# The last output tile's second product in two of 256 columns, a bank of its own for the last, and its closing scale-and-add shared by VectorE and GpSimd

## The chip, the cores and the metric

The kernel runs on the eight cores of one Trainium2 chip. Each core owns 2,048 of the 16,384 token positions and runs the same program; the cores exchange nothing. The metric is the device time of the slowest core in microseconds (us): 961.11 us is the median of three runs of the kernel before (960.91 to 961.43). The trace is one execution taken on the slowest core, which took 961.42 us in all, with a span of 959.5 us from its first to its last instruction.

## The reference

One decoder layer: a gated mixing sub-layer, then a SwiGLU feed-forward layer. The change is in the very last piece, the feed-forward layer's down projection with its normalisation and residual:

```python
def rms_norm(x, g):
    xf = x.astype(jnp.float32)
    y = xf * lax.rsqrt(jnp.mean(xf * xf, axis=-1, keepdims=True) + EPS) * g
    return y

h2 = rms_norm(x, g_pre_ffn[l])
gu = h2 @ w_gate_up[l]                       # 1024 -> 2 * 2816
a, b = gu[..., :FFN_HIDDEN], gu[..., FFN_HIDDEN:]
x = x + rms_norm((jax.nn.silu(a) * b) @ w_down[l], g_post_ffn[l])   # 2816 -> 1024
```

## The kernel before

A program written in Python lists the operations of each engine; a list scheduler with estimated costs then fixes their order and puts the waits between engines (`Prog`, its `schedule` and `emit`). Every instruction is issued from one of two lines of a helper, 521 and 523, so the rows of the trace are told apart by the names of their tiles.

The core's 2,048 positions are 16 tiles of 128. The last phase runs twice, for 8 tiles at a time: `gate_up` makes the hidden activations `ffT` (22 blocks of 128 features), then `down` makes one output tile at a time. A tile of `down` is 128 positions by 1,024 columns, made as two products of 512 columns, each a sum of 22 matmuls (`mm8` with `nk=NJ`; 16 of them take their columns from `wdna`, 6 from `wdnb`), in two neighbouring banks of PSUM, a pair from the ring `any2`. There are four such pairs.

For every tile but the last, ScalarE squares the 1,024 columns and sums them (`junkd<-ps`, then a read of the accumulator), takes a square root (`st<-st`), and VectorE multiplies the product by the gain (`x1b<-ps,gfin`), takes the reciprocal of the root and ends with one instruction that scales and adds the residual (`x1b<-x1b,st,xin`). SyncE (SP) then issues the store of 128 x 1,024 float32 values (512 KB).

For the last tile (lines 1394 to 1413) this is done in halves of 512 columns. ScalarE squares a half as soon as its product is there, VectorE multiplies it by the gain; after the second half come the square root, with the first half's sum as its bias, the reciprocal, and two scale-and-add instructions of 512 columns, columns 512 to 1,023 first. Each is followed by a store of 256 KB from SP. Nothing follows these stores: SP waits for all of the open ones and the program ends.

GpSimd (POOL) has nothing to do in the last eight tiles: its last instruction is an issue of a load of weights for `gate_up`. The scheduler's own costs hold an account of a port that VectorE and GpSimd use in turn (`n.port` in `call`, `earliest`), which sets the order only.

Of the kernel before, what the change touches and what calls it, by code (L numbers as in the profile page):

```python
# [8 lines left out]
AF = mybir.ActivationFunctionType  # L9
ALU = mybir.AluOpType  # L10
# [3 lines left out]
D = 1024  # L14
T = S // NCORES
NT = T // 128
FF = 2816
NJ = FF // 128
EPS = 1e-6
KB = 1024  # L20

MERGE_AT = 1
STATS_TO = 8
POOL_ALL = 16
FLIGHT = 5
# [547 lines left out]
def build_program():  # L573
# [26 lines left out]
    out_d = nc.dram_tensor("out", [T, D], F32, kind="ExternalOutput").ap()  # L600
# [3 lines left out]
    pe, act, dve, pool, sp = P.pe, P.act, P.dve, P.pool, P.sp  # L604
# [4 lines left out]
    def singles(ids):  # L609
        return Ring(P, [ps[:, b, :] for b in ids], [(bank[b],) for b in ids], False)  # L610

    def pairs(ids, fifo=False):
        return Ring(P, [ps[:, b:b + 2, :] for b in ids], [(bank[b], bank[b + 1]) for b in ids], fifo)

    any1, any2 = singles(range(8)), pairs([0, 2, 4, 6])
# [5 lines left out]
    def take(nbytes):  # L621
        nonlocal o
        r = o
        o += (nbytes + 31) // 32 * 32
        return r
# [15 lines left out]
    st = P.ring("st", [128, 2], F32, [take(8) for _ in range(16)], False)  # L641
# [61 lines left out]
    dsem = P.new_proc  # L703
# [64 lines left out]
    for what in LOADS:  # L768
# [17 lines left out]
        else:  # L786
            g = int(what[1])
# [25 lines left out]
    def rstd(src, junk_ring, after, by_dve=False, by_pool=False, by_act=False):  # L813

        s_, j = st.new(), junk_ring.new()
        if by_dve:
            sq = dve.scalar_tensor_tensor(out=j[:, :], in0=src, scalar=1.0, in1=src, op0=ALU.mult, op1=ALU.mult, accum_out=s_[:, 0:1], after=after)
        else:
            sq = act.activation(out=j[:, :], in_=src, func=AF.Square, accum_out=s_[:, 0:1], after=after)
        j.free(sq)  # L820
        if by_pool:
            e = pool.tensor_scalar(out=s_[:, 0:1], in0=s_[:, 0:1], scalar1=D * EPS, scalar2=None, op0=ALU.add, after=[sq])
            s_.tok = pool.tensor_tensor(out=s_[:, 1:2], in0=s_[:, 0:1], in1=nhalf[:, :], op=ALU.pow, after=[e, m_half])
        elif by_act:
            e = act.activation(out=s_[:, 0:1], in_=s_[:, 0:1], func=AF.Ln, scale=1.0, bias=D * EPS, after=[sq])
            s_.tok = act.activation(out=s_[:, 1:2], in_=s_[:, 0:1], func=AF.Exp, scale=-0.5, after=[e])
        else:
            e = act.activation(out=s_[:, 0:1], in_=s_[:, 0:1], func=AF.Sqrt, scale=1.0, bias=D * EPS, after=[sq])
            s_.tok = dve.reciprocal(out=s_[:, 1:2], in_=s_[:, 0:1], after=[e])
        return s_, sq  # L830
# [18 lines left out]
    def mm8(out, lhs, rhs, nk=8, after=(), claim=()):  # L849
        with pe.group(after) as n:  # L850
            for t in claim:
                n.tiles.append(t)
                n.after.update(t.ring.follow)
            for k in range(nk):
                pe.matmul(out, lhs(k), rhs(k), start=(k == 0), stop=(k == nk - 1))
        return n
# [117 lines left out]
    def norm_tile(i):  # L974
        halo = i >= NT
        P.bias = PART["norm_h" if halo else "norm"]
        if i % 2 == 0:
            pair[:] = [xt.pop(0), xt.pop(0)]
            sums, sqs = st4.new(), []
            for e, u in enumerate(pair):  # L980
                if e == 1 and i < STATS_TO:

# [50 lines left out]
    for g in range(4):  # L1033
        c, hf = g // 2, g % 2
# [16 lines left out]
    for c in range(2):  # L1051
        b = any1.new()
# [229 lines left out]
    for s in range(4):  # L1282
# [6 lines left out]
        pooled(s, fill1)  # L1289
        if s == MERGE_AT:  # L1290
            P.bias = PART["m01"]
# [10 lines left out]
    gfin = P.sb("gfin", [128, D], F32, R4 + 20 * KB)  # L1302
# [3 lines left out]
    junkd = P.ring("junkd", [128, D], BF16, [R3 + 32 * KB + i * 2 * KB for i in range(2)], False, follow=att_all)  # L1306
    wgu = P.ring("wgu", [128, 2, 8, 128], BF16, [R5 + i * 4 * KB for i in range(3)], follow=w01_pool)
    ffT = P.sb("ffT", [128, NJ, 1024], BF16, R2)
    wdn_a = P.sb("wdna", [128, 16, D], BF16, R1)
    wdn_b = P.sb("wdnb", [128, 6, D], BF16, R4)  # L1310
# [6 lines left out]
    v_gfin = dve.tensor_scalar(out=gfin[:, :], in0=gfin[:, :], scalar1=32.0, scalar2=None, op0=ALU.mult, after=[d_gfin])  # L1317
# [27 lines left out]
    ff_w = {0: [], 1: []}  # L1345
# [22 lines left out]
    out_evs = []  # L1368

    def down(i):  # L1370
        il = i % 8
        r = slice(i * 128, (i + 1) * 128)
        xi = xin.new()
        xi.tok = sp.dma(xi[:, :], x1s_d[r, :], after=[x1_ev[i]])
        b = any2.new()
        ms = []
        for h2 in range(2):
            ms.append(mm8(b[:, h2, :], lambda j: ffT[:, j, il * 128:(il + 1) * 128],
                          lambda j: wdn_a[:, j, h2 * 512:(h2 + 1) * 512] if j < 16 else wdn_b[:, j - 16, h2 * 512:(h2 + 1) * 512], nk=NJ, after=ff_w[i // 8] + d_wdn))
        dn_mm[i // 8].extend(ms)  # L1380
        x1 = x1b.new()
        if i < NT - 1:
            y = b.ap.rearrange("p a b -> p (a b)")
            rs, sq = rstd(y, junkd, ms, by_pool=i < NT // 2)
            g = dve.tensor_tensor(out=x1[:, :], in0=y, in1=gfin[:, :], op=ALU.mult, after=[sq, v_gfin])
            b.free(sq, g)
            w = dve.scalar_tensor_tensor(out=x1[:, :], in0=x1[:, :], scalar=rs[:, 1:2], in1=xi[:, :], op0=ALU.mult, op1=ALU.add, after=[rs.tok, g, xi.tok])
            out_evs.append(sp.dma(out_d[r, :], x1[:, :], after=[w]))
            rs.free(w)
            xi.free(w)  # L1390
            x1.free(out_evs[-1])
            return

        j, s_ = junkd.new(), [st.new(), st.new()]
        sq, g, w = [], [], []
        for h2 in range(2):
            c = slice(h2 * 512, (h2 + 1) * 512)
            sq.append(act.activation(out=j[:, c], in_=b[:, h2, :], func=AF.Square, accum_out=s_[h2][:, 0:1], after=[ms[h2]]))
            g.append(dve.tensor_tensor(out=x1[:, c], in0=b[:, h2, :], in1=gfin[:, c], op=ALU.mult, after=[sq[h2], v_gfin]))
            if h2 == 0:  # L1400
                e = dve.tensor_scalar(out=s_[0][:, 1:2], in0=s_[0][:, 0:1], scalar1=D * EPS, scalar2=None, op0=ALU.add, after=[sq[0]])
        b.free(*sq, *g)
        j.free(*sq)
        q = act.activation(out=s_[1][:, 0:1], in_=s_[1][:, 0:1], func=AF.Sqrt, scale=1.0, bias=s_[0][:, 1:2], after=[sq[1], e])
        p = dve.reciprocal(out=s_[1][:, 1:2], in_=s_[1][:, 0:1], after=[q])
        s_[0].free(q)
        for h2 in (1, 0):
            c = slice(h2 * 512, (h2 + 1) * 512)
            w.append(dve.scalar_tensor_tensor(out=x1[:, c], in0=x1[:, c], scalar=s_[1][:, 1:2], in1=xi[:, c], op0=ALU.mult, op1=ALU.add, after=[p, g[h2], xi.tok]))
            out_evs.append(sp.dma(out_d[r, c], x1[:, c], dsem("d_out%d" % h2), after=[w[-1]]))  # L1410
        s_[1].free(*w)
        xi.free(*w)
        x1.free(*out_evs[-2:])

    for i in range(NT):
        out_proj(i)
# [1 line left out]
    d_wdn = []  # L1418
    for i in range(11):
        j = 2 * i  # L1420
        dst = wdn_a[:, j:j + 2, :] if j < 16 else wdn_b[:, j - 16:j - 14, :]
        d_wdn.append(pool.dma(dst, wdn_d[:, j:j + 2, :], dsem("d_wd%d" % i), after=[wgu_n[2 * i]] + (out_mm[i // 2] if j < 16 else sum(out_mm.values(), []))))
    for i in range(8):
        down(i)
    gate_up(1)
    for i in range(8, 16):
        down(i)
# [117 lines left out]
```

How the kernel before makes its waits and increments, by code:

```python
    def emit(self):  # L480
# [19 lines left out]
                if e.seen.get(proc, 0) >= val:  # L500
                    continue
                e.seen[proc] = val
                snap = self.procs[proc].snaps.get(val)
                if snap:
                    for k, v in snap.items():
                        if e.seen.get(k, 0) < v:
                            e.seen[k] = v
                s = self.procs[proc].sem
                e.meta.append(("wait", proc, val))
                e.ops.append(lambda q, s=s, val=val: q.wait_ge(s, val))
            sem, step = (sem, 16) if n.dma else (e.proc, 1)
            sem.count += step
            n.tick = (sem.idx, sem.count)
# [2 lines left out]
            res = lambda a: a.resolve() if isinstance(a, View) else a  # L516
            for j, (method, args, kw) in enumerate(n.items):
                a = [res(x) for x in args]
                k = {q: res(x) for q, x in kw.items()}
                if j == len(n.items) - 1:
                    e.ops.append(lambda q, m=method, a=a, k=k, s=sem.sem, v=step: getattr(q, m)(*a, **k).then_inc(s, v))
                else:
                    e.ops.append(lambda q, m=method, a=a, k=k: getattr(q, m)(*a, **k))
# [1 line left out]
    def finish(self, last):  # L525
        e, need = self.sp, {}
        for n in last:
            need[n.tick[0]] = max(need.get(n.tick[0], 0), n.tick[1])
        for p, v in need.items():
            if e.seen.get(p, 0) < v:
                e.meta.append(("wait", p, v))
                e.ops.append(lambda q, s=self.procs[p].sem, v=v: q.wait_ge(s, v))
```

## Time and profile before

| | |
|---|---|
| median of three runs | 961.11 us (960.91 to 961.43) |
| the profiled execution | 961.42 us, span 959.5 us, so 1.9 us lie outside the span |
| spans of the eight cores | 955.7 to 959.5 us, mean granted clock 0.994 to 0.998 |
| busy share of the span | PE 98%, VectorE 42%, GpSimd 36%, ScalarE 34% |
| chain that ended last | PE 85%, transfers 4%, the rest 3% or less each |
| last matmul starts / last scale-and-add ends / span ends | 953.49 / 957.10 / 959.5 us |

Shares of busy time tell little here, since the change touches the last ten microseconds. What matters is the sequence of single instructions in the timeline from 948 us on: which instruction starts when, and how long after the one that it waits for.

### The profile page before, as it was taken

The numbers are of one execution on the slowest core, as the hardware profiler recorded it, in microseconds if no ns is written. First come the engines' busy times: TensorE is split into PE (matmuls) and PEld (weight loads), VectorE is DVE, ScalarE is ACT, GpSimd is POOL, SyncE is SP. The second block draws the span as 40 slices with busy tenths as digits, with TensorE's granted clock in tenths as the row PEclk, the third lists the DMA queues.
The fourth block names the chain that finished last, engine by engine and source line by source line (L and its number), as shares of the span: only waits on it lengthen the run. The fifth ranks groups of instructions, "written<-read, shape, count | busy, mean of one in ns | idle before, by whom it ended". The sixth has DMA issues, their size and how long they took to land.

```text
span 959.5 us, 15261 instructions; the slowest of 8 cores (955.7 to 959.5 us)
## 1 busy us (share of the span) xinstructions
PE 936.4 (98%) x5629; PEld 478.1 (50%) x5629; DVE 400.7 (42%) x529; ACT 321.5 (34%) x537; POOL 349.4 (36%) x358
## 2 busy tenths in 40 slices
PE   8899999999999999999999999999999999999997
PEld 4466877655554543444444444444444444444443
DVE  4578846768834653334563112221222222211323
ACT  3257524463425653234772111111011111111211
POOL 2679964467764437436891110100000000000000
PEclk9989999999999999999999999999999999999999
DMA  8996521321043228734877656652325354440221
GB/s 191 183 257 190 190 68 45 56 57 24 2 66 67 45 34 135 196 75 113 282 252 161 110 102 125 119 101 66 117 102 132 66 87 67 84 71 1 90 108 66
DMA packets 30761, 103.21 MB, mean 108 GB/s; under 512 B 4064, under 2 KB 4064, under 8 KB 30688
## 3 DMA queue, kind: packets, MB, share of 16 engines
q0 software_dynamic: 14432, 45.65, 28.9%
q1 hardware_dynamic: 15856, 56.50, 17.6%
q8 instruction: 46, 0.75, 0.3%
q14 instruction: 27, 0.22, 0.1%
q10 hardware_dynamic: 400, 0.08, 0.1%
HBM read 131.09 MB, written 16.78 MB: 154 GB/s over the span
## 4 chain that ended last, share of the span: by engine, by line
PE 85%; DMA 4%; issue 3%; ACT 3%; DVE 3%; POOL 2%; DVEq 0%; POOLq 0%; ACTq 0%; SPq 0%
PE ps L523 75%; PE ps L521 10%; DMA wgs<-wg 1%; DMA wq<-wq 1%; DMA wk<-wk 1%; DMA terms<-terms 1%; POOL x1b L521 1%; ACT PT L521 1%; DVE PT L521 1%; POOL st L521 1%; ACT L521 1%; ACT junkd L521 0%; ACT tg L521 0%; DVE x1b L521 0%; ACT den L521 0%
## 5 line engine op out<-in xcount | busy, mean ns | idle before, releaser
L523 PE MATMUL ps<-hT,wgu 128*128 128x512 bf16 x1232 | 294.6, 379 | 0.0
L523 PEld LDWEIGHTS ps<-hT,wgu 128*128 128x128 bf16 x1232 | 120.4, 98 | 144.4
L521 DVE TENSOR_TENSOR ffT<-ps,sa 128x512 bf16<-128x512 f32 x88 | 60.8, 691 | 228.9 <-PE ps L521 226.6
L521 ACT ACTIVATE sa<-ps 128x512 f32<-128x512 f32 x88 | 52.5, 596 | 238.7 <-PE ps L521 238.7
L523 PE MATMUL ps<-wdna,ffT 128*128 128x512 bf16 x512 | 115.7, 379 | 1.0 <-issue 0.6
L521 POOL DMA_DIRECT2D wgu<-wgu x44 | 23.6, 537 | 243.4 <-PE ps L521 243.4
L523 PE MATMUL ps<-hT,wgs 128*128 128x512 bf16 x448 | 108.1, 382 | 3.7 <-ACT tg L521 1.4
L521 DVE TENSOR_TENSOR rt<-ps,tab 128x512 f32<-128x512 f32 (+1 forms) x120 | 75.4, 669 | 33.7 <-PE ps L521 17.2
L523 PEld LDWEIGHTS ps<-wdna,ffT 128*128 128x128 bf16 x512 | 50.0, 98 | 61.9 <-issue 2.0
L521 ACT ACTIVATE junkd<-ps 128x1024 bf16<-128x1024 f32 (+1 forms) x33 | 32.7, 991 | 142.8 <-PE ps L521 142.7
L521 DVE SCALAR_TENSOR_TENSOR tg<-tg,ps 128x512 f32<-128x512 f32 x64 | 43.7, 686 | 75.8 <-ACT tg L521 67.5
L523 PEld LDWEIGHTS ps<-hT,wgs 128*128 128x128 bf16 x448 | 43.1, 98 | 57.0 <-issue 7.3
L521 POOL TENSOR_TENSOR k<-rt 128x512 bf16<-128x512 f32 (+1 forms) x36 | 64.9, 1817 | 17.4 <-DVE rt L521 17.0
L521 DVE TENSOR_TENSOR x1b<-ps,gfin 128x1024 f32<-128x1024 f32 (+1 forms) x17 | 19.7, 1162 | 116.9 <-ACT junkd L521 116.9
L521 PE MATMUL ps<-hT,wgu 128*128 128x512 bf16 x176 | 66.7, 379 | 0.0
L521 ACT ACTIVATE tg<-ps 128x512 f32<-128x512 f32 x64 | 38.1, 597 | 79.1 <-PE ps L521 79.0
L521 POOL TENSOR_TENSOR mT<-tg 128x512 bf16<-128x512 f32 x32 | 41.6, 1301 | 49.7 <-DVE tg L521 49.5
L521 POOL TENSOR_TENSOR q<-rt 128x512 bf16<-128x512 f32 x24 | 47.7, 2002 | 30.5 <-DVE rt L521 30.5
L521 ACT ACTIVATE PT<-ps 128x1024 bf16<-128x1024 f32 x48 | 48.8, 1022 | 28.5 <-PE ps L521 28.2
L521 DVE TENSOR_TENSOR PT<-PT,masks 128x1024 bf16<-128x1024 bf16 x48 | 46.7, 984 | 23.5 <-ACT PT L521 23.3
L523 PE MATMUL ps<-wout,mT 128*128 128x512 bf16 x224 | 53.6, 379 | 0.4 <-DVE x1b L521 0.4
L521 ACT ACTIVATE v<-ps 128x256 bf16<-128x256 f32 x69 | 26.3, 383 | 76.2 <-PE ps L521 75.8
(143 smaller groups left out, 1261.0 us busy)
## 6 DMA issues: line engine op xcount, KB each, us to landing
wgu<-wgu POOLq DMA_DIRECT2D x44, 512.0 KB, 5.2
xst<-xo SPq DMA_DIRECT2D x16, 512.0 KB, 8.5
xsth<-xh SPq DMA_DIRECT2D x16, 512.0 KB, 5.2
wgs<-wg POOLq DMA_DIRECT2D x16, 512.0 KB, 5.6
xin<-xo SPq DMA_DIRECT2D x16, 512.0 KB, 5.8
x1s<-x1b SPq DMA_DIRECT2D x16, 512.0 KB, 4.0
xin<-x1s SPq DMA_DIRECT2D x16, 512.0 KB, 4.1
out<-x1b SPq DMA_DIRECT2D x15, 512.0 KB, 2.9
```

Source lines behind the costliest of these rows:

```text
L521: e.ops.append(lambda q, m=method, a=a, k=k, s=sem.sem, v=step: getattr(q, m)(*a, **k).then_inc(s, v))
L523: e.ops.append(lambda q, m=method, a=a, k=k: getattr(q, m)(*a, **k))
```

## The change

The last tile is cut into 512, 256 and 256 columns. The products of the first two lie in the tile's pair of banks, the third in a single bank from the ring `any1`. ScalarE squares each cut apart and VectorE multiplies each by the gain; the three partial sums are added by two one-column operations and by the bias of the square root. After the reciprocal, GpSimd scales columns 0 to 191 (a `tensor_scalar`) and adds the residual (a `tensor_tensor`); VectorE does columns 608 to 1,023 and then 192 to 607 by the scale-and-add instruction, 416 columns each. There are three stores: 208 KB, 208 KB and 96 KB, issued in this order, the one of GpSimd's columns last.

```diff
+LAST_POOL = 192
...
-        for h2 in range(2):
-            ms.append(mm8(b[:, h2, :], lambda j: ffT[:, j, il * 128:(il + 1) * 128],
-                          lambda j: wdn_a[:, j, h2 * 512:(h2 + 1) * 512] if j < 16 else wdn_b[:, j - 16, h2 * 512:(h2 + 1) * 512], nk=NJ, after=ff_w[i // 8] + d_wdn))
+        cuts = [(0, 512), (512, 1024)] if i < NT - 1 else [(0, 512), (512, 768), (768, 1024)]
+        y = b.ap.rearrange("p a b -> p (a b)")
+        b2 = any1.new() if i == NT - 1 else None
+        at = [y[:, c0:c1] if c0 < 768 else b2[:, 0:256] for c0, c1 in cuts]
+        for o_, (c0, c1) in zip(at, cuts):
+            ms.append(mm8(o_, lambda j: ffT[:, j, il * 128:(il + 1) * 128],
+                          lambda j: wdn_a[:, j, c0:c1] if j < 16 else wdn_b[:, j - 16, c0:c1], nk=NJ, after=ff_w[i // 8] + d_wdn))
...
-        for h2 in range(2):
-            c = slice(h2 * 512, (h2 + 1) * 512)
-            sq.append(act.activation(out=j[:, c], in_=b[:, h2, :], func=AF.Square, accum_out=s_[h2][:, 0:1], after=[ms[h2]]))
-            g.append(dve.tensor_tensor(out=x1[:, c], in0=b[:, h2, :], in1=gfin[:, c], op=ALU.mult, after=[sq[h2], v_gfin]))
-            if h2 == 0:
+        for n, (c0, c1) in enumerate(cuts):
+            c = slice(c0, c1)
+            sq.append(act.activation(out=j[:, c], in_=at[n], func=AF.Square, accum_out=s_[n][:, 0:1], after=[ms[n]]))
+            g.append(dve.tensor_tensor(out=x1[:, c], in0=at[n], in1=gfin[:, c], op=ALU.mult, after=[sq[n], v_gfin]))
+            if n == 0:
                 e = dve.tensor_scalar(out=s_[0][:, 1:2], in0=s_[0][:, 0:1], scalar1=D * EPS, scalar2=None, op0=ALU.add, after=[sq[0]])
+            if n == 1:
+                e = dve.tensor_tensor(out=s_[1][:, 1:2], in0=s_[1][:, 0:1], in1=s_[0][:, 1:2], op=ALU.add, after=[sq[1], e])
...
-        q = act.activation(out=s_[1][:, 0:1], in_=s_[1][:, 0:1], func=AF.Sqrt, scale=1.0, bias=s_[0][:, 1:2], after=[sq[1], e])
-        p = dve.reciprocal(out=s_[1][:, 1:2], in_=s_[1][:, 0:1], after=[q])
-        for h2 in (1, 0):
-            c = slice(h2 * 512, (h2 + 1) * 512)
-            w.append(dve.scalar_tensor_tensor(out=x1[:, c], in0=x1[:, c], scalar=s_[1][:, 1:2], in1=xi[:, c], op0=ALU.mult, op1=ALU.add, after=[p, g[h2], xi.tok]))
-            out_evs.append(sp.dma(out_d[r, c], x1[:, c], dsem("d_out%d" % h2), after=[w[-1]]))
+        q = act.activation(out=s_[2][:, 0:1], in_=s_[2][:, 0:1], func=AF.Sqrt, scale=1.0, bias=s_[1][:, 1:2], after=[sq[2], e])
+        p = dve.reciprocal(out=s_[2][:, 1:2], in_=s_[2][:, 0:1], after=[q])
+        c = slice(0, LAST_POOL)
+        pa = pool.tensor_scalar(out=x1[:, c], in0=x1[:, c], scalar1=s_[2][:, 1:2], scalar2=1.0, op0=ALU.mult, op1=ALU.mult, after=[p, g[0]])
+        w.append(pool.tensor_tensor(out=x1[:, c], in0=x1[:, c], in1=xi[:, c], op=ALU.add, after=[pa, xi.tok]))
+        mid = (1024 + LAST_POOL) // 2
+        for c0, c1 in ((mid, 1024), (LAST_POOL, mid)):
+            c = slice(c0, c1)
+            w.append(dve.scalar_tensor_tensor(out=x1[:, c], in0=x1[:, c], scalar=s_[2][:, 1:2], in1=xi[:, c], op0=ALU.mult, op1=ALU.add, after=[p] + g + [xi.tok]))
+        for n, (c0, c1) in ((1, (mid, 1024)), (2, (LAST_POOL, mid)), (0, (0, LAST_POOL))):
+            out_evs.append(sp.dma(out_d[r, c0:c1], x1[:, c0:c1], dsem("d_out%d" % n), after=[w[n]]))
```

The order of all engines is the same in both kernels up to the last tile. VectorE's last rows stand so before (`x1b` is the output tile, `st` the sums, `xin` the residual, `p_scalar`, `p_vector` and `p_gpsimd` the counters of ScalarE, VectorE and GpSimd):

```order
L521 TENSOR_TENSOR x1b_113_155<-ps,gfin_147 128x512 [waits p_scalar,r84]
L521 TENSOR_SCALAR st_25_67<-st_25_67 128x1
L521 TENSOR_TENSOR x1b_113_155<-ps,gfin_147 128x512 [waits p_scalar]
L521 RECIPROCAL st_12_54<-st_12_54 128x1 [waits p_scalar]
L521 SCALAR_TENSOR_TENSOR x1b_113_155<-x1b_113_155,st_12_54,xin_109_151 128x512 [waits p_vector,r80]
L521 SCALAR_TENSOR_TENSOR x1b_113_155<-x1b_113_155,st_12_54,xin_109_151 128x512
```

And so after the change:

```order
L522 TENSOR_TENSOR x1b_113_155<-ps,gfin_147 128x512 [waits p_scalar,r85]
L522 TENSOR_SCALAR st_25_67<-st_25_67 128x1
L522 TENSOR_TENSOR x1b_113_155<-ps,gfin_147 128x256 [waits p_scalar]
L522 TENSOR_TENSOR st_12_54<-st_12_54,st_25_67 128x1 [waits p_vector]
L522 TENSOR_TENSOR x1b_113_155<-ps,gfin_147 128x256 [waits p_scalar]
L522 RECIPROCAL st_11_53<-st_11_53 128x1 [waits p_scalar]
L522 SCALAR_TENSOR_TENSOR x1b_113_155<-x1b_113_155,st_11_53,xin_109_151 128x416 [waits p_vector,r81]
L522 SCALAR_TENSOR_TENSOR x1b_113_155<-x1b_113_155,st_11_53,xin_109_151 128x416
```

The second gain product is in two pieces with a one-column add between them, and the two closing instructions have 416 columns in place of 512. On GpSimd two instructions of 192 columns follow its last load; the first waits for VectorE's counter, the second for GpSimd's own.

SP's last rows before, with its closing wait at the branch (`d_out0` and `d_out1` are the counters of the last tile's stores, `r81` to `r83` those of earlier tiles):

```order
L521 DMA out<-x1b_110_152 128x1024 [waits p_vector]
L521 DMA out<-x1b_111_153 128x1024 [waits p_vector]
L521 DMA out<-x1b_112_154 128x1024 [waits p_vector]
L521 DMA out<-x1b_113_155 128x512 [waits p_vector] x2
L563 UNCONDITIONAL_BRANCH [waits r81,r82,r83,d_out1,d_out0]
```

And after the change:

```order
L522 DMA out<-x1b_110_152 128x1024 [waits p_vector]
L522 DMA out<-x1b_111_153 128x1024 [waits p_vector]
L522 DMA out<-x1b_112_154 128x1024 [waits p_vector]
L522 DMA out<-x1b_113_155 128x416 [waits p_vector] x2
L522 DMA out<-x1b_113_155 128x192 [waits p_gpsimd]
L564 UNCONDITIONAL_BRANCH [waits r82,r83,r84,d_out1,d_out2,d_out0]
```

The third store stands behind the two of VectorE's columns in SP's queue, whichever engine is done first.

## Rows read from the trace of the kernel before

**Rows 1.** Timeline, 948 to 960 us: start, us, engine, line, operation [idle before].

```profile
948.95 3.62 PE L523 MATMUL ps<-wdna,ffT 128*128 128x512 bf16 x16
...
953.49 0.38 PE L521 MATMUL ps<-wdnb,ffT 128*128 128x512 bf16 x1
953.96 0.60 ACT L521 ACTIVATE junkd<-ps 128x512 bf16<-128x512 f32 x1 [4.06 <-PE ps L521]
954.46 0.19 ACT L521 ACTIVATION_READ_ACCUMULATOR junkd<-ps 128x1 f32 x1
954.74 0.29 ACT L521 ACTIVATE st<-st,st 128x1 f32<-128x1 f32 x1
954.75 0.69 DVE L521 TENSOR_TENSOR x1b<-ps,gfin 128x512 f32<-128x512 f32 x1 [3.93 <-ACT junkd L521]
955.36 0.15 DVE L521 RECIPROCAL st<-st 128x1 f32<-128x1 f32 x1
955.69 1.41 DVE L521 SCALAR_TENSOR_TENSOR x1b<-x1b,st,xin 128x512 f32<-128x512 f32 x2 [0.17 <-DVE st L521]
956.52 0.99 SPq L521 DMA_DIRECT2D out<-x1b  x2
```

**Rows 2.** Timeline of PE, 117 to 122 us: products of 256 columns, 8 matmuls each.

```profile
117.29 0.93 PE L523 MATMUL ps<-wv,hTh 128*128 128x256 bf16 x7
...
120.79 0.93 PE L523 MATMUL ps<-wv,hTh 128*128 128x256 bf16 x7
```

**Rows 3.** Stretches: busy of PE, PEld, DVE, ACT, POOL, then granted clock, DMA.

```profile
55.60:59.90 4.30, 4.30 (x36) 3.72 (x35) 1.29 (x2) 2.47 (x6) 4.30 (x3) 0.81 0.91 256
950.00:955.00 5.00, 3.87 (x18) 1.57 (x16) 1.00 (x3) 0.94 (x3) 0.00 (x0) 1.00 0.14 56
```

**Rows 4.** Groups by shape, whole span: busy us, mean ns | idle before.

```profile
L521 ACT ACTIVATE v<-ps 128x256 bf16<-128x256 f32 x69 | 26.3, 383 | 76.2 <-PE ps L521 75.8 <-issue 0.2
L521 DVE SCALAR_TENSOR_TENSOR x1b<-x1b,st,xin 128x1024 f32<-128x1024 f32 x15 | 19.3, 1284 | 3.1 <-DVE x1b L521 1.9 <-DVE st L521 1.2
L521 DVE SCALAR_TENSOR_TENSOR x1b<-x1b,st,xin 128x512 f32<-128x512 f32 x2 | 1.4, 747 | 0.2 <-DVE st L521 0.2
L521 POOL TENSOR_SCALAR xsb<-xsth,st 128x1024 bf16<-128x1024 f32 x16 | 17.7, 1120 | 1.2 <-ACT st L521 1.0
L521 POOL TENSOR_TENSOR x1b<-x1b,xin 128x1024 f32<-128x1024 f32 x16 | 37.4, 2351 | 4.0 <-DVE x1b L521 4.0
L521 POOL TENSOR_TENSOR k<-rt 128x128 bf16<-128x128 f32 x2 | 0.9, 450 | 1.9 <-DVE rt L521 1.9
```

**Rows 5.** Timeline of VectorE and GpSimd, 198 to 226 us.

```profile
198.29 0.17 DVE L521 TENSOR_TENSOR uZ<-uZ,small 64x16 f32<-64x16 f32 x1
...
208.30 1.06 POOL L521 TENSOR_TENSOR uY<-uX 128x527 f32<-128x527 f32 x1 [1.26 <-DVE zT L521]
209.04 0.35 DVE L521 TENSOR_TENSOR uZ<-uZ,small 64x16 f32<-64x16 f32 x1
...
221.21 2.26 POOL L521 TENSOR_TENSOR q<-rt 128x512 bf16<-128x512 f32 x1
221.60 2.42 DVE L521 TENSOR_TENSOR PT<-PT,masks 128x1024 bf16<-128x1024 bf16 x1
```

**Rows 6.** Timeline, 276 to 278 and 661 to 663 us: when GpSimd starts.

```profile
276.62 0.69 DVE L521 SCALAR_TENSOR_TENSOR tg<-tg,ps 128x512 f32<-128x512 f32 x1 [0.20 <-ACT tg L521]
277.46 1.26 POOL L521 TENSOR_TENSOR mT<-tg 128x512 bf16<-128x512 f32 x1 [1.00 <-DVE tg L521]
...
661.33 0.22 POOL L521 TENSOR_SCALAR st<-st 128x1 f32<-128x1 f32 x1 [12.30 <-ACT junkd L521]
...
661.70 0.57 POOL L521 TENSOR_TENSOR st<-st,nhalf 128x1 f32<-128x1 f32 x1
```

**Rows 7.** DMA issues: count, KB each, median us from issue to landing.

```profile
out<-x1b SPq DMA_DIRECT2D x15, 512.0 KB, 2.9
out<-x1b SPq DMA_DIRECT2D x2, 256.0 KB, 2.1
```

More of the change, by code:

```diff
@@ L1382, in down @@
         if i < NT - 1:
-            y = b.ap.rearrange("p a b -> p (a b)")
             rs, sq = rstd(y, junkd, ms, by_pool=i < NT // 2)
@@ L1392, in down @@
             return
-        j, s_ = junkd.new(), [st.new(), st.new()]
+        j, s_ = junkd.new(), [st.new(), st.new(), st.new()]
         sq, g, w = [], [], []
-        for h2 in range(2):
-            c = slice(h2 * 512, (h2 + 1) * 512)
-            sq.append(act.activation(out=j[:, c], in_=b[:, h2, :], func=AF.Square, accum_out=s_[h2][:, 0:1], after=[ms[h2]]))
-            g.append(dve.tensor_tensor(out=x1[:, c], in0=b[:, h2, :], in1=gfin[:, c], op=ALU.mult, after=[sq[h2], v_gfin]))
-            if h2 == 0:
+        for n, (c0, c1) in enumerate(cuts):
[3 more added lines that the diff above has]
+            if n == 0:
@@ L1401, in down @@
                 e = dve.tensor_scalar(out=s_[0][:, 1:2], in0=s_[0][:, 0:1], scalar1=D * EPS, scalar2=None, op0=ALU.add, after=[sq[0]])
-        b.free(*sq, *g)
+            if n == 1:
+                e = dve.tensor_tensor(out=s_[1][:, 1:2], in0=s_[1][:, 0:1], in1=s_[0][:, 1:2], op=ALU.add, after=[sq[1], e])
+        b.free(*sq[:2], *g[:2])
+        b2.free(sq[2], g[2])
         j.free(*sq)
-        q = act.activation(out=s_[1][:, 0:1], in_=s_[1][:, 0:1], func=AF.Sqrt, scale=1.0, bias=s_[0][:, 1:2], after=[sq[1], e])
@@ L1405, in down @@
-        p = dve.reciprocal(out=s_[1][:, 1:2], in_=s_[1][:, 0:1], after=[q])
-        s_[0].free(q)
-        for h2 in (1, 0):
-            c = slice(h2 * 512, (h2 + 1) * 512)
-            w.append(dve.scalar_tensor_tensor(out=x1[:, c], in0=x1[:, c], scalar=s_[1][:, 1:2], in1=xi[:, c], op0=ALU.mult, op1=ALU.add, after=[p, g[h2], xi.tok]))
-            out_evs.append(sp.dma(out_d[r, c], x1[:, c], dsem("d_out%d" % h2), after=[w[-1]]))
-        s_[1].free(*w)
+        q = act.activation(out=s_[2][:, 0:1], in_=s_[2][:, 0:1], func=AF.Sqrt, scale=1.0, bias=s_[1][:, 1:2], after=[sq[2], e])
@@ new lines, in down @@
+        p = dve.reciprocal(out=s_[2][:, 1:2], in_=s_[2][:, 0:1], after=[q])
+        s_[0].free(e)
+        s_[1].free(q)
+        c = slice(0, LAST_POOL)
[5 more added lines that the diff above has]
+            w.append(dve.scalar_tensor_tensor(out=x1[:, c], in0=x1[:, c], scalar=s_[2][:, 1:2], in1=xi[:, c], op0=ALU.mult, op1=ALU.add, after=[p] + g + [xi.tok]))
@@ L1412, in down @@
+        for n, (c0, c1) in ((1, (mid, 1024)), (2, (LAST_POOL, mid)), (0, (0, LAST_POOL))):
+            out_evs.append(sp.dma(out_d[r, c0:c1], x1[:, c0:c1], dsem("d_out%d" % n), after=[w[n]]))
+        s_[2].free(*w)
         xi.free(*w)
-        x1.free(*out_evs[-2:])
+        x1.free(*out_evs[-3:])
     for i in range(NT):
```

## The prediction

> **What bounds the kernel now.** I read the stretches first: from 950 to 955 us PE is busy to the last matmul, at a granted clock of 1.00, the level of 2.4 GHz [rows 3]. So the last tile starts when PE comes to it, and nothing that is changed lies ahead of that. Then I read the timeline of the end, where every step is a wait for the step before [rows 1]. The second product's 22 matmuls start at 948.95 and the last of them at 953.49, 4.54 / 21 = 0.216 us apart; it takes 0.38 us, and ScalarE starts its square at 953.96, 0.09 us after that end. The accumulator is read 0.50 us after the start of the square. From this read the square root starts 0.28 us later and VectorE's gain product 0.29 us later, side by side. The reciprocal starts at 955.36, 0.08 us before the gain product's end at 955.44 and long after the root's end at 955.03, so VectorE's own queue sets it. It ends at 955.51, and 0.18 us later the two scale-and-add instructions start; they end at 957.10. SP issues the first store at 956.52, which is 0.08 us after the first of them (0.747 us, [rows 4]) has ended at 956.44, and the second one the same 0.08 us after 957.10, at 957.18. SP is done at 957.51, so an issue takes 0.33 us. A store of 256 KB lands 2.1 us after its issue [rows 7], at 959.28. From the last matmul to that landing there are 5.4 us of bare waiting, and these are what the change works on. I set its sum against 959.28 in this execution of 961.42 us, which is 0.31 us above the median of 961.11.
>
> **The change part by part.**
>
> *The product in two.* 22 matmuls of 512 columns become 44 of 256. Five products of 256 columns with 8 matmuls each ran back to back early in the kernel: the first began at 117.29, the fifth at 120.79, so 32 matmuls took 3.50 us, 0.1094 us each [rows 2]. Half of 0.216 is 0.108, so the weight load before each matmul stays hidden and little is lost. The last of the 44 starts 43 x 0.1094 = 4.70 us after 948.95, at 953.65. A matmul of 512 columns takes 0.38 us from its start, of 256 columns about 0.11 less, 0.27, so the sum is there at 953.92 in place of 953.87: 0.05 us lost. The middle product's square, gain product and one-column add have the 2.4 us of the third product to run in; the matching work on the first half takes from 953.96 to 955.44 when nothing hides it [rows 1], so they cost nothing. Without that cover they would cost their 1.5 us. The third product's bank was used by one of the tiles before, whose reads end microseconds earlier.
>
> *The last square and gain product.* With 256 columns ScalarE takes 0.383 us [rows 4] against 0.60: 0.22 less. Square from 954.01, accumulator read at 954.01 + 0.50 - 0.22 = 954.29, gain product at 954.58, root from 954.57 to 954.86. VectorE's price per column is (1284 - 747) / 512 = 1.05 ns [rows 4], so its product takes 0.69 - 0.27 = 0.42 us and ends at 955.00. The reciprocal could start at 954.92 by VectorE's queue, but the root's end at 954.86 plus the 0.10 us that VectorE takes to hear ScalarE (954.65 to 954.75, [rows 1]) makes it 954.96. It ends at 955.11, 0.40 us earlier than before. From here on I count from 955.11.
>
> *The shared end.* VectorE's instruction of 416 columns takes 0.747 - 0.10 = 0.65 us, two in a row 0.56 + 0.65. GpSimd's two are shown at no width of 192. The scale lies between 0.21 us (192/1024 of 1.120) and 0.39 (0.22 for one column plus 191 x 0.88 ns) [rows 4, 6]; I take 0.39, since a fixed part is plain in the one-column row. The add lies between 0.44 us (192/1024 of 2.351) and 0.59 (0.45 for 128 columns plus 64 x 2.12 ns) [rows 4]; I take 0.59, since 128 is the nearest width. GpSimd starts 0.15 us after an instruction of VectorE that it waits for (277.31 to 277.46), and 0.15 us after one of its own (661.55 to 661.70) [rows 6]. The scale could thus start at 955.26 and VectorE's first instruction at 955.11 + 0.18 = 955.29.
>
> They can't run together. At 209.04 VectorE starts an instruction with two inputs in SBUF while GpSimd works: it takes 0.35 us where the same takes 0.17, and ends 0.03 us after GpSimd's 209.36. At 221.60 another takes 2.42 us and ends 0.55 us after the GpSimd instruction that was running, at 223.47 [rows 5]. Such an instruction waits for the whole GpSimd instruction, apart from some 0.13 us of its beginning. And at 221.21 GpSimd, waiting for a VectorE instruction, went ahead of the next one of VectorE's queue, which was started at 221.60 [rows 5]. So whoever has waited goes next. The scale-and-add reads `x1b` and `xin`, both in SBUF, so it is such an instruction, and the two engines take turns.
>
> The Trainium skill, GPSIMD Engine Reference, section Key points, says that GpSimd shares its SBUF interfaces with VectorE and contends with VectorE instructions that have two SBUF inputs; these rows agree. By that rule alone the end is the one with turns below, without it the one without turns.
>
> With GpSimd first: scale 955.26 to 955.65; VectorE's first ends 0.52 later at 956.17; GpSimd's add, ready at 955.80, ends 0.59 - 0.14 = 0.45 later, at 956.62; VectorE's second ends at 957.14. SP issues the second store at 957.22 and the third, which stands behind it, 0.33 later at 957.55. With VectorE first: 955.94, scale 956.20, second 956.72, add 957.17; second store at 956.80, third at 957.25. The starts are 0.03 us apart, which decides nothing, so I take both orders as one case.
>
> *The stores.* The third has 96 KB. By the step from 512 to 256 KB (0.8 us less, [rows 7]) it would land in 2.1 - 0.5 = 1.6 us; it can hardly take more than the 2.1 of 256 KB. I take 1.8. It lands at 957.55 + 1.8 = 959.35 or at 959.05, against 959.28: +0.07 or -0.23, and with the bounds of the landing -0.43 to +0.37. The second store, with 208 KB, would land by the same step at 957.22 + 1.95 = 959.17, before the third.
>
> *Sum:* +0.05 for the product, -0.45 for square, gain product and the earlier reciprocal, and then a shorter VectorE end that is given back by the turns and by a third issue on SP. The middle of the two orders is -0.08 us: 961.34 against 961.42, and 961.0 against the median. The forecast is no change that can be measured; 0.2%, 1.9 us here, is about what a measurement of this kernel can tell from no change.
>
> **The rivals.**
>
> *No turns.* If instructions of this kind don't exclude each other, VectorE ends at 955.29 + 0.56 + 0.65 = 956.50 and GpSimd at 955.26 + 0.39 + 0.15 + 0.59 = 956.39. The second store goes at 956.58, the third at 956.91, and lands at 958.71: 0.57 us faster, 960.5. For it: none of my rows has a float32 scale-and-add of this form beside GpSimd. Against it: the 0.35 us row is float32 with two inputs in SBUF, and the rule is plain in it.
>
> *The product slows down.* The matmuls of 256 columns could fall to a lower granted clock in the last tile. Its place is 951 to 954 us. Where products of 256 columns ran at a granted 0.81 [rows 3], the price per matmul is 0.1094 / 0.81 = 0.135 us, 0.026 more, and 44 of them add 1.1 us: 962.1, slower than before. At the level of 1.2 GHz it would be 4.8 us: 965.8, a slowdown that is measurable. It decides as soon as the granted clock between 949 and 954 us is under about 0.98, where 44 x 0.002 us takes up the gain of 0.08. For it: it did happen at 55.6. Against it: there it was in the first tenth of the run, and here the clock is 1.00 up to the end.
>
> *The change doesn't do what it says.* The order shows the 44 matmuls, the two GpSimd instructions and the three stores, in their places. I give this nothing.
>
> **How the numbers follow.** Turns on the port 0.78 (961.0, and 960.7 to 961.5 by its own bounds), no turns 0.14 (960.5), a slower product 0.08, of which 0.03 at the level of 1.2 GHz. Runs of the kernel before differ by 0.5 us among themselves, so I add 0.3 us on either side of the cases that I take in: 960.3 to 961.8. Faster by over 0.2% needs a gain of 1.9 us, and no case has it: 0.01. Slower by over 0.2%: 0.03. The rest, 0.96, is within.
>
> **What would show it.** In the timeline after: 44 matmuls 0.109 us apart; the last square some 0.38 us long; the reciprocal about 0.4 us closer to the start of the second product; then one scale-and-add, or GpSimd's scale, longer than its 0.65 or 0.39 us by the other's time, and a third store issued 3.6 to 3.9 us after the last matmul's start (here 953.65). It is wrong if both engines' closing instructions keep their plain durations side by side, if the matmuls stand 0.13 us apart, or if the third store's landing takes more than 2.1 us.

## The result and the profile after

The changed kernel takes 967.47 us (median of four runs, 967.15 to 968.95) against 961.01 us before: a ratio of 1.0067, 95% interval 1.0056 to 1.0079. It is slower by 6.5 us, where no measurable change (961.0, range 960.3 to 961.8) was forecast. Medians of one kernel move by about a microsecond from one measuring session to the next, so every comparison below goes by the ratio to the kernel before in the same session, or by one core's trace. The ratios leave out executions in which the cores of a die showed a lower granted clock and the time was longer.

The timeline of the changed kernel's end, on its slowest core (start us, us, engine, line, operation; all line numbers are one higher than before):

```profile
948.55 1.91 PE L524 MATMUL ps<-wdna,ffT 128*128 128x256 bf16 x16
...
953.25 0.27 PE L522 MATMUL ps<-wdnb,ffT 128*128 128x256 bf16 x1
953.62 0.38 ACT L522 ACTIVATE junkd<-ps 128x256 bf16<-128x256 f32 x1 [1.93 <-PE ps L522]
953.90 0.20 ACT L522 ACTIVATION_READ_ACCUMULATOR junkd<-ps 128x1 f32 x1
954.19 0.29 ACT L522 ACTIVATE st<-st,st 128x1 f32<-128x1 f32 x1
954.20 0.42 DVE L522 TENSOR_TENSOR x1b<-ps,gfin 128x256 f32<-128x256 f32 x1 [1.91 <-ACT junkd L522]
954.58 0.16 DVE L522 RECIPROCAL st<-st 128x1 f32<-128x1 f32 x1
954.92 1.30 DVE L522 SCALAR_TENSOR_TENSOR x1b<-x1b,st,xin 128x416 f32<-128x416 f32 x2 [0.17 <-DVE st L522]
954.93 0.86 POOL L522 TENSOR_SCALAR x1b<-x1b,st 128x192 f32<-128x192 f32 x1 [98.33 <-DVE st L522]
955.65 1.47 SPq L522 DMA_DIRECT2D out<-x1b  x3
955.99 0.67 POOL L522 TENSOR_TENSOR x1b<-x1b,xin 128x192 f32<-128x192 f32 x1 [0.21 <-POOL x1b L522]
```

These rows answer to [rows 1], and up to GpSimd's end they are close to what was forecast. The product of columns 512 to 1,023, now in two parts, starts at 948.55; the reciprocal comes 954.58 - 948.55 = 6.03 us after that, where it came 955.36 - 948.95 = 6.41 us after it: 0.38 us earlier, forecast 0.40. GpSimd ends at 956.66. The three stores land after these times (KB each, median us from issue to landing, to be read beside [rows 7]):

```profile
out<-x1b SPq DMA_DIRECT2D x2, 208.0 KB, 1.9
out<-x1b SPq DMA_DIRECT2D x1, 96.0 KB, 1.8
```

The last issue ends at 955.65 + 1.47 = 957.12 and so starts near 956.75; it lands 1.8 us later, at 958.5, which is 5.3 us after the last matmul's start. Before it was 5.8; yet the last matmul starts 4.70 us after the start of the product, where it was 4.54, so only 0.3 us of the 0.5 are gained. But the span ends at 965.3. The table of SP's waits (what was waited for: us in total, times, longest) shows that the time is lost after the stores:

```profile
SPq L564 <- PEq L564: 6.7, 1, 6.7
SPq L534 <- DMA out<-x1b: 1.1, 3, 0.6
```

SP waits 1.1 us for the stores and then 6.7 us at line 564, where the program's end is built. In the kernel before that wait was 0.2 us:

```profile
SPq L563 <- PEq L563: 0.2, 1, 0.2
```

The engine named there, PE, had long been done; which one it really was stands in the instructions of that line (operation: shortest/median/longest ns, first and last start us). After the change:

```profile
L564 POOLq EVENT_SEMAPHORE  x2: 17/17/17, 965.1 to 965.2; - x2
L564 PEldq DRAIN  x1: 2155/2155/2155, 951.4 to 951.4; - x1
L564 ACTq DRAIN  x1: 306/306/306, 954.2 to 954.2; - x1
L564 DVEq DRAIN  x1: 1282/1282/1282, 955.0 to 955.0; - x1
L564 POOLq DRAIN  x1: 9119/9119/9119, 956.0 to 956.0; - x1
L564 SPq DRAIN  x1: 7/7/7, 958.6 to 958.6; - x1
L564 SPq EVENT_SEMAPHORE  x1: 17/17/17, 965.3 to 965.3; - x1
```

And in the kernel before, at its line 563:

```profile
L563 POOLq EVENT_SEMAPHORE  x2: 17/17/17, 959.3 to 959.4; - x2
L563 POOLq DRAIN  x1: 9410/9410/9410, 856.5 to 856.5; - x1
L563 SPq DRAIN  x1: 7/7/7, 959.3 to 959.3; - x1
```

At the program's end a DRAIN instruction stands in the queue of every engine, and the engines meet when all of them are through (the EVENT_SEMAPHORE rows). In these traces GpSimd's closing drain starts together with its last instruction. Before, that was a load of weights, 103 us before the end, and the drain of 9.4 us lay beside PE's matmuls of `gate_up`. Now the last instruction is the add at 955.99; the drain takes 9.12 us from there, on this core as on all others within 2 ns, which is the add's own 0.67 us and 8.45 us more, and the engines of the core meet at 965.1. The drain didn't appear with the change: it was pulled to the end by it.

### The profile page after: what moved, and what is told of

The parts are those of the page before. It is cut to its first block, busy times and chain, and to the rows that moved or that the text cites. A ratio compares the mean times of both kernels' runs of the same rounds, so it can differ in the third digit from the quotient of the medians.

```text
span 965.3 us, 15227 instructions; the slowest of 8 cores (958.4 to 965.3 us)
## 1 busy us (share of the span) xinstructions
PE 927.6 (96%) x5557; PEld 478.5 (50%) x5651; DVE 402.8 (42%) x531; ACT 321.7 (33%) x539; POOL 351.4 (36%) x360
## 3 DMA queue, kind: packets, MB, share of 16 engines
q0 software_dynamic: 14432, 45.65, 28.9%
## 4 chain that ended last, share of the span: by engine, by line
PE 79%; DMA 6%; issue 5%; ACT 4%; POOL 3%; DVE 3%; POOLq 0%; ACTq 0%; DVEq 0%; SPq 0%
PE ps L524 69%; PE ps L522 10%; DMA wq<-wq 2%; DMA wv<-wv 1%; DMA wk<-wk 1%; DMA wgs<-wg 1%; POOL x1b L522 1%; ACT PT L522 1%; DVE PT L522 1%; POOL st L522 1%; DMA xst<-xo 1%; ACT L522 1%; POOL xsb L522 1%; ACT junk L522 0%; ACT junkd L522 0%
## 5 line engine op out<-in xcount | busy, mean ns | idle before, releaser
L524 PE MATMUL ps<-hT,wgu 128*128 128x512 bf16 x1203 | 290.8, 379 | 1.2
L524 PE MATMUL ps<-wdna,ffT 128*128 128x512 bf16 (+1 forms) x517 | 115.2, 372 | 1.5 <-issue 0.6
L522 ACT ACTIVATE junkd<-ps 128x1024 bf16<-128x1024 f32 (+2 forms) x34 | 32.9, 967 | 142.3 <-PE ps L522 142.3
L522 DVE TENSOR_TENSOR x1b<-ps,gfin 128x1024 f32<-128x1024 f32 (+2 forms) x18 | 19.9, 1106 | 116.1 <-ACT junkd L522 116.1
L522 PE MATMUL ps<-hT,wgu 128*128 128x512 bf16 x176 | 66.7, 379 | 0.3
```

The source lines that it names most:

```text
L522: e.ops.append(lambda q, m=method, a=a, k=k, s=sem.sem, v=step: getattr(q, m)(*a, **k).then_inc(s, v))
L524: e.ops.append(lambda q, m=method, a=a, k=k: getattr(q, m)(*a, **k))
```

## The experiments

The theory, **A**: the 6.5 us are GpSimd's drain, which follows its last instruction and can now hide behind nothing. The rivals: **B**, the products of 256 columns or the third bank cost it; **C**, the turns at the port and the third store do.

How long each kernel's slowest core takes from the start of its last matmul to the end of its span, beside the ratio to the kernel before:

| kernel | last matmul to end, us | ratio, 95% interval |
|---|---|---|
| before | 6.0 | |
| changed | 12.1 | 1.0067 (1.0056 to 1.0079) |
| without GpSimd's part | 5.5 | 0.9985 (0.9975 to 0.9996) |
| before, tiny instruction late | 10.2 | 1.0036 (1.0022 to 1.0049) |
| before, the same early | 6.1 | 0.9999 (0.9988 to 1.0009) |
| changed, end without the drain | 5.6 | 0.9989 (0.9978 to 1.0001) |
| before, end without the drain | 6.1 | 0.9998 (0.9983 to 1.0013) |
| without GpSimd's part and drain | 5.6 | 0.9988 (0.9974 to 1.0002) |
| changed, one more drain early | 5.7 | 0.9985 (0.9971 to 0.9999) |
| changed, one more drain halfway | 5.5 | one run of each: 959.35 beside 960.62 us |

Where the product is in two, the last matmul starts 0.16 us later after the product's start than before. So 0.16 us of what such a kernel has less than the 6.0 in the middle column is no gain.

**Without GpSimd's part.**

```diff
-        pa = pool.tensor_scalar(out=x1[:, c], ...)
-        w.append(pool.tensor_tensor(out=x1[:, c], ...))
...
-        for c0, c1 in ((mid, 1024), (LAST_POOL, mid)):
...
-            w.append(dve.scalar_tensor_tensor(out=x1[:, c], ...))
-        for n, (c0, c1) in ((1, (mid, 1024)), (2, (LAST_POOL, mid)), (0, (0, LAST_POOL))):
-            out_evs.append(sp.dma(out_d[r, c0:c1], ...))
+        for n, (c0, c1) in ((1, (512, 1024)), (0, (0, 512))):
+            w.append(dve.scalar_tensor_tensor(out=x1[:, c0:c1], ...))
+            out_evs.append(sp.dma(out_d[r, c0:c1], x1[:, c0:c1], dsem("d_out%d" % n), after=[w[-1]]))
...
```

> The products in 256 columns and the separate bank stay; GpSimd's two instructions go, VectorE does both closing halves of 512 columns, two stores of 256 KB. Theory A (the 6.5 us are GpSimd's drain at the end of the program, which now starts only after GpSimd's last instruction): GpSimd's drain lies around 856 us again and is over long before the end, and the time is 960.5 to 960.7 us, 0.3 to 0.5 us under the kernel before. Theory B (the shorter matmuls or the third bank cost the time): it stays near 967 us. Theory C (the exchange of the port between VectorE and GpSimd and the third store cost it): near 961 us, so this run alone does not tell A from C.

It is 0.15% faster than the kernel before (960.40 us beside 961.49), 1.4 us by the ratio with an interval of 0.4 to 2.4, where 0.3 to 0.5 was expected. Its end (instructions of line 564, then the last matmul in the timeline):

```profile
L564 POOLq DRAIN  x1: 9399/9399/9399, 857.5 to 857.5; - x1
L564 SPq DRAIN  x1: 7/7/7, 960.0 to 960.0; - x1
```

```profile
954.68 0.27 PE L522 MATMUL ps<-wdnb,ffT 128*128 128x256 bf16 x1
```

B falls: the 44 matmuls and the third bank are all in here. The drain is back at 857 us. SP is done 960.0 - 954.68 = 5.3 us after the last matmul's start. A and C are not told apart yet.

**A tiny GpSimd instruction, late and early.** The kernel before with one instruction of one column on GpSimd, which nobody reads or waits for:

```diff
         s_[0].free(q)
+        t_ = st.new()
+        t_.free(pool.tensor_scalar(out=t_[:, 0:1], in0=nhalf[:, :], scalar1=D * EPS, scalar2=None, op0=ALU.add, after=[sq[1], m_half]))
```

In the second kernel it is released by `sq[0]`, the square of the first half.

> The kernel before, with one GpSimd instruction of one column added, released by the last square; nothing reads its result, no engine waits for it, the stores are unchanged. Theory A: it runs about 1.0 us after the last matmul's start plus 0.2, so GpSimd's drain ends about 8.5 us later, some 4 us after the last store has landed: the time is 964.5 to 965.5 us. Theories B and C: no change, 961.0 us within 0.3.

> The same added instruction, but released by the square of the first half, 4.7 us earlier. Theory A: the drain ends 8.5 us after it, at or just before the landing of the last store, so the time is that of the kernel before, 961.0 to 961.3 us. If the mere presence of a late GpSimd instruction cost a fixed time wherever it stands, it would be as slow as the one released late.

Late, it costs 0.36% (964.96 us beside 961.49); early, nothing. In the kernel with the late one (timeline, then the instructions of its line 563):

```profile
956.50 0.38 PE L521 MATMUL ps<-wdnb,ffT 128*128 128x512 bf16 x1
957.83 0.22 POOL L521 TENSOR_SCALAR st<-nhalf 128x1 f32<-128x1 f32 x1 [97.81 <-ACT junkd L521]
```

```profile
L563 POOLq DRAIN  x1: 8681/8681/8681, 957.8 to 957.8; - x1
L563 SPq DRAIN  x1: 7/7/7, 962.3 to 962.3; - x1
```

SP is done with the stores at 962.3, and the drain ends at 957.83 + 8.68 = 966.5. With the early one:

```profile
949.91 0.22 POOL L521 TENSOR_SCALAR st<-nhalf 128x1 f32<-128x1 f32 x1 [93.06 <-ACT junkd L521]
```

```profile
L563 POOLq DRAIN  x1: 8681/8681/8681, 949.9 to 949.9; - x1
L563 SPq DRAIN  x1: 7/7/7, 959.1 to 959.1; - x1
```

The drain is as long, 8.46 us after the instruction's 0.22, but ends at 958.6, half a microsecond before SP is done. One instruction of 0.2 us that no one waits for costs 3.5 us (4.2 in the trace: 10.2 in place of 6.0) in one place and nothing 4.7 us earlier. This is A alone; there is no sharing, no third store and no shorter matmul in these kernels.

**The end without the drain.** Both kernels, with the engines meeting by semaphores and GpSimd not drained:

```diff
-        with nc.Block() as block:
+        with nc.Block(no_gpsimd_drain=True) as block:
```

> The changed kernel, every instruction kept, but the program's end is built without GpSimd's drain: the engines meet by semaphores alone. Theory A: the 6.5 us go, and what is left is the sum of the prediction's own parts: 960.3 to 960.8 us. Theories B and C: it stays at 967 us.

> The kernel before, with the program's end built without GpSimd's drain. Its drain of 9.4 us lies at 856 us and is over 93 us before the end, so Theory A says no change: 961.0 to 961.5 us, the same as the kernel before within 0.1%. If it were faster by a microsecond or more, the gain of the changed kernel without the drain would be the option's own and not the drain's.

The changed kernel falls from 1.0067 to 0.9989; the kernel before stays at 0.9998. So the option brings nothing of its own, and the whole loss of the change goes with the drain. At the end of the changed kernel without it (timeline, then its line 564):

```profile
954.89 0.27 PE L522 MATMUL ps<-wdnb,ffT 128*128 128x256 bf16 x1
```

```profile
L564 POOLq EVENT_SEMAPHORE  x2: 17/17/17, 960.3 to 960.4; - x2
L564 SPq DRAIN  x1: 7/7/7, 960.2 to 960.2; - x1
```

SP is done 5.3 us after the last matmul's start, as in the kernel without GpSimd's part. C falls, since the turns and the third store are all in here; but so does the use of sharing: it brings nothing over VectorE alone that these traces can show.

**Without GpSimd's part and without the drain.** This joins the edits of the first and of the last experiment.

> Products of 256 columns, no GpSimd work at the end, two stores, and the program's end without GpSimd's drain. Theory A: the same as with the drain, since that lies at 857 us: 960.4 to 960.8 us, 0.3 to 0.6 us under the kernel before. It shows what of the gain is left to the shared end: the changed kernel without the drain has its last landing 5.3 us after the last matmul's start, this one should have 5.5.

The ratio is 0.9988, with an interval that just holds 1. Its end (timeline, then its line 564):

```profile
954.33 0.27 PE L522 MATMUL ps<-wdnb,ffT 128*128 128x256 bf16 x1
```

```profile
L564 SPq DRAIN  x1: 7/7/7, 959.6 to 959.6; - x1
```

SP is done 5.3 us after the last matmul's start, where 5.5 was expected: with and without the sharing the stores are in at the same time. The kernel isn't told apart from the other three with the new products and no long drain left at the end (called repaired below), 0.9985 to 0.9989.

**One more drain, early and halfway.** What is the 8.4 us? The changed kernel with a drain of its own on GpSimd where it has nothing else to do:

```diff
     gate_up(1)
+    dr = pool.drain(after=[wgu_n[-1]])
```

(The scheduler's own cost for a drain, added in this kernel and the next one, is left out here.)

> The changed kernel with one more GpSimd drain in its program, behind the last load of weights that GpSimd issues, some 90 us before the end, where GpSimd has nothing else to do; the drain at the end stays. Theory A1 (the drain's 8.46 us wait for or clear what GpSimd's own transfers have left since the last drain): the second drain is a few tenths of a us long, like the 0.17 us of the one at the program's start, and the time is 960.5 to 961.0 us. Theory A2 (each drain of GpSimd costs 8.46 us once the program has issued transfers from it): no change against the changed kernel, 967 us.

The extra drain and the one at the end (instructions of lines 524 and 566 on the slowest core):

```profile
L524 POOLq DRAIN  x1: 8396/8396/8396, 864.5 to 864.5; - x1
...
L566 POOLq DRAIN  x1: 764/764/764, 959.2 to 959.2; - x1
```

The drain at the end is down to 0.764 us, 0.09 more than the add that it stands behind, and the kernel is at 0.9985. A1 holds, with a correction: the extra drain starts at 864.5, when the last load (issued at 859.3, 5.2 us to its landing) has landed, and still takes 8.4 us. So these 8.4 us are no wait for a landing. What the drain does in them no run shows. Whether they go with the number of transfers is asked by a kernel with the drain put before `gate_up(1)`:

```diff
+    dr = pool.drain(after=[wgu_n[21]] + d_wdn)
+    dr.prio = -1
     gate_up(1)
```

> The changed kernel with the extra drain of GpSimd put earlier, behind 81 of the 102 transfers that GpSimd issues, so that 21 are issued after it and have long landed at the end. If the drain's price goes with the number of transfers since the last drain (8.4 us for 102, 0.083 us each), the extra drain takes 6.7 us and the one at the end 1.7 us after the last add, which hides behind the last store: about 960.7 us. If it is one price however many there were, both take 8.4 us after what stands before them and the time is 967 us.

```profile
L524 POOLq DRAIN  x1: 7427/7427/7427, 634.4 to 634.4; - x1
...
L566 POOLq DRAIN  x1: 2497/2497/2497, 954.9 to 954.9; - x1
```

The drain at the end takes 2.497 - 0.67 = 1.83 us after the add, with 21 transfers since the last drain. With none it was 0.09, with all 102 it was 8.45: (1.83 - 0.09) / 21 = 0.083 us and (8.45 - 0.09) / 102 = 0.082 us for each. The price goes with the number of transfers, in one run of this kernel, whose eight cores agree within 1 ns on the 2.497 us. It doesn't go with their bytes. The page of this run has GpSimd's queue (packets, MB, share of the DMA engines' time):

```profile
q0 software_dynamic: 14432, 45.65, 28.6%
```

The 21 carry 512 KB each, 11.0 of these 45.65 MB, and by that share the drain would have taken 2.11 us after the add. Whether it is the transfers or the packets they are made of isn't told apart. The extra drain was to take 6.7 us and took 7.4, on other cores 7.2 to 8.8; it started when a load issued at 633.3 was still under way, and how much of it is waiting for that isn't separated.

## Why the prediction was wrong

The step that failed is the first one: "From the last matmul to that landing there are 5.4 us of bare waiting, and these are what the change works on. I set its sum against 959.28 ..." It took the landing of the last store for the end of the program. The sum thus has no term for what the program does between its last instructions and its end, and on GpSimd that is a drain of 8.4 us. The move of GpSimd's last instruction from 856 to 956 us was put at nothing, without a reason: it takes away the cover of everything that follows that instruction on its engine, and I named no such thing. What I wrote of the kernel before has the same gap: "Nothing follows these stores" and "Every instruction is issued from one of two lines of a helper" leave out the drains and semaphores of line 563. The evidence lay in the trace of before, in the instructions of that line; I read the end from the timeline, which shows no drains, and read GpSimd's queue only up to its last instruction. No rival held it: the slower one was a slower product, and the chance left for a measurable slowdown was 0.03. Of the three signs of being wrong that I named none came; none of them looked behind the stores.

The terms that were in the sum, counted from the last matmul's start:

- The product in two: the matmuls are (953.25 - 948.55) / 43 = 0.109 us apart, as worked out. Right. The granted clock was 1.00 in the stretches 940 to 950 and 950 to 955 us, the level of 2.4 GHz, so the slow product didn't come.
- Square, gain product, reciprocal: the square takes 0.38 us and the gain product 0.42, both as forecast; the reciprocal starts after 1.33 us, forecast 1.31.
- The turns: VectorE's first closing instruction goes first. SP issues its store at 955.65, so by the 0.08 us of [rows 1] it ends at 955.57 and took the forecast 0.65 us. GpSimd's scale starts 0.01 us behind it, takes 0.86 in place of the estimated 0.39, and ends at 955.79, 0.22 after it (forecast 0.26). VectorE's second ends at 956.22, 0.43 after that (forecast 0.52), and GpSimd's add at 956.66, 0.44 later (forecast 0.45). That is the case "with VectorE first", each step within 0.1 us; it put the add's end 3.52 us after the last matmul's start, it was 3.41. The rule of the Trainium skill (GPSIMD Engine Reference, section Key points), that the two engines contend when VectorE's instruction has two inputs in SBUF, agrees with these numbers. No run has GpSimd's scale or add of 192 columns without VectorE beside it, so how much longer the turns made them rests on the estimates.
- The third store: issued 3.50 us after the last matmul's start, just under the 3.6 to 3.9 that were named, and 1.8 us to land, forecast 1.8. SP is done after 5.3 us, forecast 5.4 for this order.

So up to the stores the sum had the mechanism right; what it took for the end was not the end. From the start of the product of columns 512 to 1,023 until SP is done with the stores it is 958.6 - 948.55 = 10.05 us, before it was 959.3 - 948.95 = 10.35: a gain of 0.3, where the sum had 0.08 as the middle of two orders and 0.23 for the one that came. The repaired kernels gain 0.2 to 0.4 by the same count. The forecast of "no measurable change" holds for the change without the drain (0.9989, interval 0.9978 to 1.0001). The times of the repaired kernels lie 1.1 to 1.4 us under the kernel before, with intervals of about 1 us to either side; whether more than the 0.3 is real these traces don't show. What was missing is one term: SP's wait at the closing line, 6.7 us in place of 0.2.

## What to carry to other kernels

Before work is given to an idle engine near the end, look at what follows that engine's last instruction up to the program's end; what is hidden behind an early finish becomes part of the path when the finish moves. A busy share or a timeline of compute instructions doesn't show it: read the instructions of the line that ends the program, on each engine. If GpSimd has issued transfers and must work late, drain it once in an idle stretch after its last transfer (a ratio of 0.9985 in place of 1.0067 here), or keep its last instruction well ahead of the end.

## What the runs showed of the hardware

GpSimd's drain in these kernels takes 0.09 us plus 0.082 to 0.083 us for each transfer that GpSimd has issued since its last drain, 8.4 us for 102, even when the last of them was issued 100 us before; this goes by three points, with 0, 21 and 102 transfers. A scale of 192 columns on GpSimd that starts 0.01 us after VectorE's float32 scale-and-add of 416 columns, which has two inputs in SBUF, takes 0.86 us and ends 0.22 us after it; alone it was estimated at 0.39, and no run has it alone.
